# Hybrid decoder step: the sample's attention moved from the front to between tile 0's U rows, part two's merge and queries moved behind it

## What is computed

```python
xn = rmsnorm(x); u, cq, ckv, kr, qx, gates = split(xn @ w_in)
pool_y = grouped trailing means of u
mla_o  = latent attention: 8 heads, latent 256 wide, rope 32 wide
         prompt: causal over 512; sample: over 16 pages of 128 past tokens
         of each sequence, found by page_table, and the 4 new tokens
mem_o  = 4-head attention into 256 memory tokens (sample: cached, per sequence)
h = x + (g0*(pool_y @ w_pool_out) + g1*(mla_o @ w_mla_out) + g2*(mem_o @ w_x_out)) @ w_o
# expert layer: 8 heads x 16 experts of 16384 for every token
q = rmsnorm(h) @ w_peer_q; 128 expert ids and gates per token from two top-16
a = gelu(h . peer_u[ids]); y = h + (gates * a) @ peer_v[ids]; final rmsnorm
```

## Time and profile before

| | us |
|---|---|
| median of 3 runs | 2352.08 |
| lowest, highest | 2350.12, 2361.64 |
| the profiled execution | 2363.59 |
| its span, first to last instruction | 2361.9 |
| busy in it: PE, DVE, POOL, ACT | 1303.4, 1167.5, 1099.9, 260.8 |

### The profile page before, as it was taken

The page is one execution under the profiler, slowest core; times in us unless marked ns, Lnnn a source line. Parts: engine busy times, 40 slices in busy tenths (PEclk is TensorE's granted clock), DMA queues, the critical chain, the costliest instruction groups (busy, mean ns, idle before and its releaser), DMA issues.

```text
span 2361.9 us, 21631 instructions
## 1 busy us (share of the span) xinstructions
PE 1303.4 (55%) x6930; PEld 791.1 (33%) x6930; DVE 1167.5 (49%) x2824; ACT 260.8 (11%) x655; POOL 1099.9 (47%) x1226
## 2 busy tenths in 40 slices
PE   7997888999897657778820155400055400045513
PEld 5875545788785435434510011000011100001100
DVE  2104324511158876655298773188775088840060
ACT  2213223610120000011100000000000000000000
POOL 0004500000025434666566666666666666666664
PEclk9998897999999778889965577655577755567756
DMA  6214634055469889999999999999999999999997
GB/s 200 72 64 133 169 99 125 1 163 134 134 205 375 302 286 353 394 390 392 387 387 373 357 360 356 366 393 373 370 335 366 362 396 366 371 351 368 362 389 261
DMA packets 323510, 687.44 MB, mean 291 GB/s; under 512 B 37111, under 2 KB 174232, under 8 KB 323391
## 3 DMA queue, kind: packets, MB, share of 16 engines
q0 software_dynamic: 161792, 579.94, 65.3%
q1 hardware_dynamic: 161607, 106.13, 15.5%
HBM read 681.84 MB, written 4.18 MB: 290 GB/s over the span
## 4 chain that ended last, share of the span: by engine, by line
PE 28%; DVE 24%; POOL 11%; issue 11%; another core or an unknown queue 11%; DMA 7%; SPq 4%; DVEq 1%; ACT 1%; ACTq 0%
PE bank L671 21%; DVE arena L1872 20%; POOL arena L638 11%; DMA arena<-in_peer_v_dram,arena 5%; PE bank L1156 3%; PE bank L667 2%; DVEq L1808 1%; DMA arena<-in_w_pool_out_dram 1%; SPq L503 1%; SPq L507 1%; SPq L504 1%; PE bank L1013 1%; DMA arena<-in_peer_u_dram,arena 1%; PE bank L1131 0%
## 5 line engine op out<-in xcount | busy, mean ns | idle before, releaser
L638 POOL DMA_INDIRECT arena<-in_peer_u_dram,arena x544 | 510.7, 939 | 714.2 <-DVE arena L1856 382.5
L671 PE MATMUL bank<-arena 128*128 128x256 f32 (+7 forms) x2940 | 704.7, 397 | 102.7 <-DVE arena L1774 29.4
L1872 DVE CUSTOM_DVE_ANT_0 arena<-arena,bank 128x1024 f32<-128x1024 f32 x544 | 637.0, 1218 | 59.8 <-issue 55.4
L638 POOL DMA_INDIRECT arena<-in_peer_v_dram,arena x544 | 515.5, 948 | 295.3 <-issue 136.3
L671 PEld LDWEIGHTS bank<-arena 128*128 128x128 f32 (+2 forms) x2940 | 542.1, 193 | 264.2 <-issue 114.7
L1156 PE MATMUL bank<-arena 128*32 128x512 f32 x2176 | 384.5, 839 | 350.7 <-DMA arena<-in_peer_v_dram,arena 276.5
L667 PE MATMUL bank<-arena 128*128 128x128 f32 (+5 forms) x774 | 127.8, 313 | 560.5 <-issue 320.9
L667 PEld LDWEIGHTS bank<-arena 128*128 128x128 f32 (+5 forms) x774 | 106.1, 162 | 600.6 <-issue 362.0
L1156 PEld LDWEIGHTS bank<-arena 128*32 128x32 f32 x2176 | 84.6, 135 | 625.5 <-issue 621.6
L1901 DVE TENSOR_TENSOR arena<-arena,bank 128x1024 f32<-128x1024 f32 x5 | 6.1, 1221 | 377.0 <-PE bank L1156 222.9
L1192 ACT ACTIVATE arena<-bank 128x256 f32<-128x256 f32 (+12 forms) x325 | 126.4, 418 | 454.4 <-PE bank L671 192.4
(11 more groups left out here) (146 smaller groups left out, 751.9 us busy)
## 6 DMA issues: line engine op xcount, KB each, us to landing
arena<-in_w_in_dram SPq DMA_DIRECT2D x48, 512.0 KB
arena<-in_w_peer_q_dram SPq DMA_DIRECT2D x32, 512.0 KB
arena<-in_peer_u_dram,arena POOLq DMA_INDIRECT x544
arena<-in_peer_v_dram,arena POOLq DMA_INDIRECT x544
arena<-in_cache_kv_latent_dram POOLq DMA_DIRECT2D x64, 128.0 KB
arena<-in_cache_kv_latent_dram SPq DMA_DIRECT2D x64, 128.0 KB, 2.2
arena<-in_w_o_dram SPq DMA_DIRECT2D x8, 1024.0 KB, 11.0
arena<-in_w_in_dram SPq DMA_DIRECT2D x6, 1024.0 KB
```

The source lines that it names most:

```text
L638: pool.indirect_dma_start(out=ring[s % RING], out_offset=None, in_=table[0], in_offset=IndirectOffsetOnAxis(ap=ix, axis=0)).then_inc(land[ ...
L671: last = pe.matmul(dst, lhs(k), rhs(k), start=(k == 0), stop=(k == n - 1))
L1872: dve.tensor_tensor_reduce(ring[s % RING], ring[s % RING], h_dot, 1.0, 0.0, ALU.mult, ALU.add, act_a[:, p % 2, k:k + 1]).then_inc(u_free, 1)
```

## The change

The sample's attention leaves the front. It becomes a generator `sample()` on TensorE, ScalarE and DVE, ahead of `part(1)` in the same background. Its steps are half as wide: 2 pages for 4 sequences, 16 steps of 3 units; TensorE uses banks 4 and 5 in turn for the page turns (ScalarE alone empties them), bank 6 for scores, bank 7 for probabilities and values. All page loads are on SP now, behind part one's query loads; POOL's loop is gone. The memory attention follows, with two load buffers and 10 rounds of 2 units. Operands that the front's later work would overwrite (new latents, sample queries, masks) are copied on ScalarE to a place of their own, and w_uv is loaded a second time. `zw`, whose place the steps use, is cleared ahead of gather 124, behind a wait for the last output turn. The 48 half units of part two's merge are due from tick 147 to 273 (V block 0 and a little of U block 1), w_o, norms and turns at ticks 278 to 326, the queries at 330 to 381, all in U block 1 (ticks 256 to 383).

```diff
-PGRP = 4
+PGRP = 2
...
 def background_ticks():
 
-    u0, v0 = PLACE["u", 0, 0], PLACE["v", 0, 0]
-    ticks = [u0 + 2 + 5 * h // 2 for h in range(2 * MERGE)]
-    ticks += [v0 + 4 * r + 3 for r in range(12)]
-    ticks += [v0 + 52 + 2 * t for t in range(3)]
-    ticks += [v0 + 62 + 4 * t for t in range(3)]
-    ticks += [v0 + 76 + 4 * j for j in range(QJ + 2)]
+    u0, u1 = PLACE["u", 0, 0], PLACE["u", 1, 0]
+    ticks = [u0 + 3 + 23 * i // 12 for i in range(3 * (STEPS + 1))]
+    ticks += [u0 + 102 + 2 * i for i in range(3)]
+    ticks += [u0 + 109 + 7 * i // 4 for i in range(2 * (NB + 2))]
+    ticks += [u0 + 147 + 27 * h // 10 for h in range(2 * MERGE)]
+    ticks += [u1 + 22 + 27 * r // 10 for r in range(12)]
+    ticks += [u1 + 56 + 2 * t for t in range(3)]
+    ticks += [u1 + 64 + 3 * t for t in range(3)]
+    ticks += [u1 + 74 + 3 * j for j in range(QJ + 2)]
     return ticks
 
...
-        lat = [at(115.75 + 18 * i, [4, PGRP, KL]) for i in range(3)]
-        rop = [at(131.75 + 18 * i, [PGRP, P]) for i in range(3)]
...
-        smem = at(151.75, [4, 2, 2, 512])
...
+        qxs = at(19.25, [XH, NS])
+        paged = [119, 163, 172]
+        lat = [at(a, [4, PGRP, KL]) for a in paged]
...
+
...
-                i, a, g = s % 3, s // 4, s % 4
-                if s == 2:
-                    sp.wait_ge(pool_mm, 2 * PG)
-                    sp.wait_ge(pool_d, PG)
+                i, a, g = s % 3, s // HALVES, s % HALVES
                 if s >= 3:
                     sp.wait_ge(pv_mm, s - 2)
-                for j in range(2):
+                elif s >= 1:
+                    sp.wait_ge(pq_mm, QJ)
+                for j in range(4):
+                    n = (4 * a + j) * PAGES + g * PGRP
...
+                        page = sp.value_load(pagetab[0:1, n + k:n + k + 1], min_val=0, max_val=cache_lat.shape[1] - 1)
...
-            sp.wait_ge(ld_gain, 16 * 13)
-            for s in range(STEPS):
-                load_pages(s)
-
-            for b in range(NB):
-                if b == 0:
-                    sp.wait_ge(pv_mm, 6)
-                elif b == 2:
-                    sp.wait_ge(ps_mm, STEPS)
-                elif b >= 4:
-                    sp.wait_ge(mo_mm, b - 3)
-                    sp.wait_ge(mt_mm, 2 * (b - 3))
+            def load_memory(b):
+                if b < 2:
+                    sp.wait_ge(pv_mm, STEPS - 2 + b)
+                else:
+                    sp.wait_ge(mo_mm, b - 1)
+                    sp.wait_ge(mt_mm, 2 * (b - 1))
                 for k, src in enumerate((cache_mk, cache_mv)):
-                    sp.dma_start(smem[:, b % 4, k], src[0, b].rearrange("(m p) h e -> p m (h e)", p=P)).then_inc(
-                        ld_smem[b % 4], 16)
+                    sp.dma_start(smem[b % 2][:, k], src[0, b].rearrange("(m p) h e -> p m (h e)", p=P)).then_inc(
+                        ld_smem[b % 2], 16)
 
...
                 if n >= 4:
                     sp.wait_ge(mg_mm, MERGE * g + n - 3)
                 elif g == 0:
+                    sp.wait_ge(pool_mm, 2 * PG)
+                    sp.wait_ge(pool_d, PG)
+                elif n < 3:
+                    sp.wait_ge(mo_mm, (NB - 1, NB, NB)[n])
+                    sp.wait_ge(mt_mm, 2 * NB)
+                else:
+                    sp.wait_ge(so_mm, 1)
                     sp.wait_ge(mo_mm, NB)
-                else:
-                    sp.wait_ge(pq_mm, (12, 13, 15, 16)[n])
...
+            sp.wait_ge(ld_gain, 16 * 13)
+            for s in range(STEPS):
+                load_pages(s)
+                if s == 1:
+                    sp.dma_start(wuvs[:], w_uv[0].rearrange("(k p) h e -> p k (h e)", p=P)).then_inc(ld_wuv, 16)
+            for b in range(NB):
+                load_memory(b)
+            sp.wait_ge(pv_mm, STEPS)
+            sp.dma_start(gfin[:], final_norm.rearrange("(a d) -> a d", a=1).to_broadcast([P, D])).then_inc(ld_gain, 16)
             for n in range(MERGE):
...
-            pool.wait_ge(ld_gain, 16 * 13)
-            pool.wait_ge(qt_mm, 2 * TILES)
-            for s in range(STEPS):
-                i, a, g = s % 3, s // 4, s % 4
...
-                if s >= 3:
-                    pool.wait_ge(pv_mm, s - 2)
-                for j in range(2, 4):
-                    for k in range(PGRP):
...
                 if s == 0:
                     pool.wait_ge(stored, 16 * 3)
-                if s == 8:
+                if s == 124:
...
+            def page_turns(s):
+
+                i = s % 3
+                pe.wait_ge(ld_page[i], 16 * 16 * (s // 3 + 1))
...
+                    if n >= 2:
+                        pe.wait_ge(pt_ev, n - 1)
+                    for k in range(2 * PGRP if u < 4 else PGRP):
+                        if u < 4:
+                            c, page = k // PGRP, k % PGRP
+                            src = lat[i][:, u, page, c * P:(c + 1) * P]
+                        else:
+                            src = rop[i][:, k]
+                        last = turn(bank[:, 4 + n % 2, k * P:(k + 1) * P], src, P)
+                    last.then_inc(pt_mm, 1)
...
+            def page_probs(s):
+
+                a, g = s // HALVES, s % HALVES
+                pe.wait_ge(ps_exp, s + 1)
+                if s >= 1:
+                    pe.wait_ge(pv_ev, s)
+                if s == HALVES:
+                    pe.wait_ge(po_ev, 1)
+                for k in range(PGRP):
+                    last = turn(bank[:, 7, k * P:(k + 1) * P], prob[:, s % 2, k * P:(k + 1) * P], P)
+                if g == HALVES - 1:
+                    last = turn(bank[0:NS, 6, 3 * P:4 * P], probn[:, a], P)
+                last.then_inc(pp_mm, 1)
...
+            def mem_turns(b):
+                pe.wait_ge(ld_smem[b % 2], 32 * (b // 2 + 1))
+                for i in range(2):
+                    if b >= 1:
+                        pe.wait_ge(mt_ev, 2 * b - 1 + i)
+                    for k in range(4):
+                        h, m = 2 * i + k // 2, k % 2
+                        last = turn(bank[:, 4 + i, k * P:(k + 1) * P],
+                                    smem[b % 2][:, 0, m, h * XD:(h + 1) * XD], P)
+                    last.then_inc(mt_mm, 1)
...
+            def mem_values(b):
+                pe.wait_ge(mp_ev, b + 1)
+                if b >= 1:
+                    pe.wait_ge(mx_ev, b)
+                for m in range(2):
+                    for h in range(XH):
+                        last = pe.matmul(bank[32 * h:32 * h + TS, 7, 256:256 + XD], smpT[:, m, 32 * h:32 * h + TS],
+                                         smem[b % 2][:, 1, m, h * XD:(h + 1) * XD], start=(m == 0), stop=(m == 1))
+                last.then_inc(mo_mm, 1)
...
+                for s in range(STEPS + 1):
+                    if s == HALVES + 1:
+                        page_out(0)
+                    if s < STEPS:
+                        page_turns(s)
+                    yield
+                    if s >= 1:
+                        page_probs(s - 1)
+                    if s < STEPS:
+                        page_scores(s)
+                    yield
+                    if s >= 1:
+                        page_values(s - 1)
+                    yield
+                page_out(1)
+                yield
+                pe.wait_ge(po_ev, 2)
...
+                yield
+                pe.wait_ge(bank_zero, 2)
+                for n in range(NB + 2):
+                    if n >= 2:
+                        mem_out(n - 2)
+                    if n < NB:
+                        mem_turns(n)
+                    if 1 <= n <= NB:
+                        mem_probs(n - 1)
+                    yield
+                    if n < NB:
+                        mem_scores(n)
+                    if 1 <= n <= NB:
+                        mem_values(n - 1)
+                    yield
+                pe.wait_ge(mx_ev, NB)
...
                 pass
-            bg = Background(part(1))
+            bg = Background(joined(sample(), part(1)))
             for p in range(TILES):
                 u = PLACE["u", p, 0]
                 if p < TILES - 1:
-                    bg.advance(u + (112 if p == 0 else 0))
+                    bg.advance(u + (111 - LAG if p == 0 else 0))
                     turn_ids(p)
-                    bg.advance(u + P - 1)
+                    bg.advance(u + P - 1 - LAG)
                     turn_weights(p)
...
+            copy(cnew[:], cT[:, :, SEQ:NT])
+            copy(cnewt[0:NS], cqkv[0:NS, 0, QL:QL + KL])
+            copy(qxs[:], qxT[:, :, SEQ:NT])
             for n in range(KV_UNITS):
...
+                    if s < STEPS:
+                        for u in range(5):
+                            act.wait_ge(pt_mm, 5 * s + u + 1)
+                            if s >= 1:
+                                act.wait_ge(ps_mm, s)
+                            src = bank[:, 4 + (5 * s + u) % 2]
+                            if u < 4:
+                                copy(latT[:, u].rearrange("p a b -> p (a b)"), src).then_inc(pt_ev, 1)
```

(32 more changed lines are left out.)

602 lines of the change are left out of this document (233 added, 369 removed).

## The result

The changed kernel takes 2411.82 us (median of 4 runs, 2407.09 to 2422.03) beside 2352.15 us for the kernel before (4 runs): a ratio of 1.0251, 95% interval [1.0207, 1.0296]. It is slower by 60 us where 56 us less were forecast. The profiled execution has a span of 2420.1 us against 2361.9; both profiled executions are some 10 us longer than their medians.

A forecast was written before the change was run, and what follows sets the result against it. Chain length was taken to bound the front, DMA bytes nearly everything behind it; -155 + 17 + 38 + 44 = -56 us from 2352 gave 2296 us, own range 2280 to 2315, ends 2262 and 2350.

The forecast's parts named there:

- Part 1: Front, before the first product: sample work leaves the chain ahead of the prompt scores, -155 us (bounds -150 and -160).
- Part 2: U block 0: gains sample steps and memory units, loses 24 merges; waits for pages, +17 us (bounds -11 and +107).
- the price of a page pair: SP's page issue in U block 0: 1.85 us a pair, 14.8 us a step; bounds 1.61 and 2.6 us a pair.
- the slower rival: U block 0: page queue starves behind gathers, 2.6 us a pair, block +107, total 2386 us; chance 0.09.
- SP's queue is the limit: U block 0: SP issuing all 256 page DMAs, not VectorE's work, sets the pace; VectorE and rows wait for pages.
- Part 3: V block 0: memory units with two buffers, then merges led by DMA, 235 us against 197, +38 us.
- The stop of the memory units: V block 0, behind the first quads: seven memory units at 10.5 us each come due in a row, some 38 us.
- Part 4: U block 1: added merge weights, w_o, x rows and 16 query loads cost DMA time, +44 us (bounds +30 and +60).
- it fits down to a clock of 0.7: U block 1: TensorE's own work, 150 us at full clock, fits within the block's 219 us.
- the price of a query load: U block 1: 1.4 us of DMA for each of 16 query loads.
- that rule: Page loads in U block 0: DMA engines serve queues in turn, several descriptors a packet, so pages could stand behind gathers.
- Later blocks: From V block 1 on: everything as before, 0 us; a difference of more than 5 us would show the forecast wrong.

The follow-up runs named there:

- pause in tile 0's rows: GpSimd clears a small tile after each tile 0 U gather: 0.9861 on the combined edits with split memory loads, 0.9939 on the kernel before.
- units in the picks: Changed kernel with the sample units of 8 more rows done inside picks 2 and 3: ratio 1.0228; also without page loads from step 3: 1.0135.
- splitting them: Memory keys' and values' loads wait separately, added to six gathers ahead, paired query loads, queries in V block 1 and units inside picks: 2351.89 us, 0.994.
- pause 24: Changed kernel with GpSimd clearing 256 numbers after each gather in tile 1's U rows, 12 gathers ahead still allowed: ratio 1.0149, U block 1 248.1 us.
- six ahead: Changed kernel with at most 6 instead of 12 gathers ahead of the products in tile 1's U rows: ratio 1.0154, U block 1 240.0 us.
- VectorE's waits: Changed kernel with VectorE waiting in U block 1, at query unit j, until the scores of query j-3 are copied: ratio 1.0101, U block 1 230.6 us.
- query loads in pairs: Changed kernel with six gathers ahead in tile 1's U rows and part two's query weights loaded two at a time in 1 KB rows: 2379.93 us, 1.0104.

## Why the prediction was wrong, step by step

**Part 1** (-155) was right in mechanism: part one's last query but one starts on TensorE at 542.9 where it started at 695.3, 152 us earlier. The last one ends only 145 us earlier (558.0 against 702.9) and the first product comes 147 us earlier, since TensorE and the pick ahead of the product are held up. TensorE, VectorE and GpSimd in the changed kernel:

```profile
546.57 0.38 PE L662 MATMUL bank<-arena 128*128 128x256 f32 x1 [0.28 <-issue]
548.67 0.27 PE L1116 MATMUL bank<-arena 128*128 128x128 f32 x1 [1.72 <-issue]
550.77 0.37 PE L1116 MATMUL bank<-arena 128*128 128x128 f32 x1 [1.83 <-issue]
...
545.86 0.94 POOL L628 DMA_INDIRECT arena<-in_peer_u_dram,arena  x1 [0.30 <-issue]
545.91 0.29 DVE L1789 MAX8 arena<-arena 128x8 f32<-128x128 f32 x1 [1.05 <-issue]
...
549.41 0.09 DVE L1791 MATCH_VALUE_LOAD arena<-arena 128x8 f32 x1 [2.42 <-issue]
...
551.51 0.29 DVE L1792 MAX8 arena<-arena 128x8 f32<-128x128 f32 x1 [1.75 <-issue]
```

TensorE goes on by one matmul every 2.1 us, and VectorE has idle times of 1.05, 2.42 and 1.75 us put down to "issue", behind the first 12 gathers, issued 1.24 us apart: the sign of U block 1, now on VectorE too. From the first gather to the first product it is 31 us in every run without a pause in tile 0's rows and 25.9 with it. In the kernel before it is 26.5: there the clearing of `zw` breaks the row ahead of gather 8, and the change moved it away. That the clearing did it is likely but was not tried.

**Part 2** (+17, measured +73) had the price of a page pair right: means of 1.65 to 1.92 us in 13 of 15 steps (2.56 and 2.04 in the others), where 1.85 was taken and 2.3 would have made the slower rival. That rival did not happen either; the time went elsewhere. Steps 1 to 15 took 248 us of SP, 16.5 a step instead of 14.8, by two stops, at picks 2 and 3, where ScalarE waits for the pick's result ahead of the next copies (ScalarE and SP):

```profile
648.28 0.23 ACT L1444 ACTIVATE arena<-arena 128x32 f32<-128x32 f32 x1 [17.70 <-DVE arena L1815]
...
648.66 0.33 SPq L509 DMA_DIRECT2D arena<-in_cache_k_rope_dram  x1
667.66 0.01 SPq L506 DMA_DIRECT2D arena<-in_cache_kv_latent_dram  x1
```

The step of the prediction that failed is the sentence that SP's queue is the limit: with no page loads from step 3 on the block still took 289 us, where 267 were forecast with all of them. I compared VectorE's work and SP's issues as two rates and took the larger. But a unit passes through TensorE, ScalarE and VectorE several times, and each passage waits for its place in three fixed orders; without pages and with units in the picks VectorE still waits 67 us in the block (106 in the changed kernel, 41 in the kernel before). Some of it, 12 us of the block (the run with the pause in tile 0's rows), is the hold-up by gathers; the rest I can only name as the chain of the units, since no run took it apart. Behind the last page (807) the last steps' chain took 20 us instead of 12, and the rest of the block 62 instead of 43, with VectorE waiting 12 and 4 us for memory scores. So the 56 us beyond the forecast are 26 in SP's steps, 8 in that chain, 19 in the rest, and 3 because the pages started 7 instead of 10 us ahead of the first product.

**Part 3** (+38, measured +52) was right in mechanism. The stop of the memory units in V block 0 shows as the window 888.5 to 930 above, 41.5 us at a DMA share of 0.49 where 38 were forecast; the merge phase took 207.6 us at a share of 1.05 where 200 were. Of the 14 us beyond the forecast the merges are 8, the stop 3 and the rounding of 238 to 235 another 3. That the two buffers' waits are real is shown by splitting them, which returned 21 us over both blocks.

**Part 4** (+44, measured +92) failed in the sentence "it fits down to a clock of 0.7". It weighed TensorE's 150 us against 219 and priced the loads by bytes, and had no term for TensorE and ScalarE not going on at all. The old trace could have shown it, in the one place where queries and an unbroken row of gathers met: the idle times of 27 and 31 us in the old U block 1, shown above. The prediction read that block by its window, in which TensorE has little work, and in the old V block 0, where most queries stood, the gathers waited for TensorE. The hold-up was worth 24 to 42 us of the block (pause 24, six ahead 32, VectorE's waits 42), and 23 to 35 us by the ratios. The second, smaller failure is the price of a query load, 1.4 us of DMA by its bytes; 16 loads of 1,024 rows of 512 bytes cost the block 18 us more than 8 loads of 1,024 rows of 1 KB, the same bytes (12 us by the ratios), and one such load stood 10.9 us in the queue. The Trainium skill ("DMA: Bandwidth & Descriptors", Queues, rings and completion order) says that an engine serves its queues in turn, a packet at a time. The counts of 1033 and 1032 packets agree as to the turns; by them it is one row a turn on either side, and not several, as the prediction had it from that section. The prediction weighed that rule on the pages and not on the query loads; the pages came sooner than it would have them, but only 32 gathers were issued in the first 82.5 us of U block 0, so the gather queue was not always full there. With both failures out of the way (six ahead, query loads in pairs) U block 1 took 221.9 us, where 180 + 44 = 224 were forecast.

**Later blocks** came out 11 us shorter, where I wrote that more than 5 us would be wrong. The runs that leave these blocks as they are show 1003 to 1016 us there, the kernel before with the pause in tile 0's rows 1016, so much of it is scatter between traces and chips; that all of them lie under the 1018 of before stays unexplained.

The sum of the misses: 8 in front, 56 in U block 0, 14 in V block 0, 48 in U block 1, less 11: 115 us. The range went to 2350, 54 us above the forecast; it left out the slower rival, the only place where +107 in U block 0 was allowed.

## What to carry to other kernels

A block in which one engine streams and the others are idle tells nothing of whether work fits beside it: look for a stretch of the trace, however short, in which the two really run together at that pace, and at every idle time in it, also on engines for which nobody waits. Here 30 us of the old U block 1 would have done. Idle times called "issue" or "remote" that grow behind an unbroken row of GpSimd gathers are worth one small experiment, a pause of 0.2 us in each gather. Price a load that stands beside a full gather queue by its rows, not by its bytes. And where several engines pass a unit to and fro in fixed orders, compare the length of a unit's chain with its schedule, not only each engine's rate; an engine that blocks for another's result (ScalarE at the pick) stops everything behind it.

## What the runs showed of the hardware

- With indirect gathers issued by GpSimd every 1.24 us in an unbroken row, TensorE went on by one matmul each 2.1 or 2.8 us and ScalarE started a ready copy up to 40 us late (26 us in the kernel before); VectorE's pick had idle times up to 2.4 us. At 1.43 us a gather the single matmuls and the waits of 20 to 40 us were gone. Half of the bytes (DMA share 0.71) or half of VectorE's work left them there. Why is open.
- While a load and the gathers both stood in their queues, the DMA engines took as many packets from one as from the other, rows of 512 bytes beside rows of 4 KB (1032 and 1033 in 10.9 us; 3751 and 3752 in 40 us). Loads of 0.52 MB in rows of 512 bytes so came through among the gathers at one in 11 us (in the run with the pause, queries that waited for them started at 1308.5 and, the fourth after it, at 1352.6), where their bytes are 1.4 us of DMA; the same bytes in 1 KB rows took 18 us off the block (12 by the ratios).
- TensorE's clock followed its work, not the reverse: 0.61 in the 65 us in which it was held up, 1.00 in 31 us of the same place with six gathers ahead.
